# Two layer norms of a two-block transformer kernel rewoven: sums and centring from PSUM, a root by ScalarE, low parts by GpSimd alone, half-slab waits for TensorE

## What is computed

```python
x = _layer_norm(ALPHA * x + gate1 * y, ln1_g, ln1_b)        # y ends with "@ w_out"
h = x * (1.0 + scale2) + shift2
u = depthwise_conv3(h @ w_up) + conv_b                      # 5632 channels
gate, val = split(u, 2)
y = (silu(gate) * val) @ w_down
x = _layer_norm(ALPHA * x + gate2 * y, ln2_g, ln2_b)        # the output

def _layer_norm(x, g, b):
    mu = mean(x, -1); var = mean(square(x - mu), -1)
    return (x - mu) * rsqrt(var + 1e-5) * g + b
```

## Time and profile before

| | |
|---|---|
| median of 3 runs | 1785.66 us (1785.66 to 1786.78) |
| the profiled execution, its own time | 1783.52 us |
| its span, first to last instruction | 1781.4 us |
| mean granted PE clock | 0.997 |
| PE busy | 1748.0 us, 98% of the span |
| DVE, ACT, POOL busy | 972.4, 677.6, 825.1 us |
| DMA | 178.49 MB, 100 GB/s on average |

### The profile page before, as it was taken

How to read it: one execution, slowest core, us unless ns; L and a number is a source line. 1 busy time by engine, 2 the same in 40 slices (tenths; PEclk the granted TensorE clock), 3 DMA queues, 4 the chain that set the end, 5 groups by cost and what they waited for, 6 DMA issues and landing times. The chain is left out here.

```text
span 1781.4 us, 26139 instructions
## 1 busy us (share of the span) xinstructions
PE 1748.0 (98%) x8971; PEld 1485.4 (83%) x8971; DVE 972.4 (55%) x1592; ACT 677.6 (38%) x1399; POOL 825.1 (46%) x664
## 2 busy tenths in 40 slices
PE   8999999999999999999999999999999899999997
PEld 6888888888777888888888888999988878888886
DVE  4266535668975477252124359475577673551544
ACT  5322222243476433233233223665532552332333
POOL 4554454467971555544445555201034465444551
PEclk9999999999999999999999999999999999999999
DMA  7354452534312345433423333100022134323321
GB/s 230 108 180 138 142 154 83 179 96 116 89 34 60 117 142 184 145 95 95 124 78 100 107 95 99 44 1 25 1 59 83 48 101 136 101 88 107 94 83 48
DMA packets 279716, 178.49 MB, mean 100 GB/s; under 512 B 6280, under 2 KB 258372, under 8 KB 279492
## 3 DMA queue, kind: packets, MB, share of 16 engines
q1 hardware_dynamic: 265364, 149.35, 28.8%
q10 hardware_dynamic: 14256, 27.87, 4.5%
HBM read 175.11 MB, written 2.10 MB: 99 GB/s over the span
## 5 line engine op out<-in xcount | busy, mean ns | idle before, releaser
L655 POOL TENSOR_TENSOR wL<-raw,wH 128x512 fp32r<-128x512 f32 (+2 forms) x560 | 747.5, 1358 | 889.8 <-ACT wH L1443 798.9
L761 PE MATMUL ps<-actH,wH 128*128 128x512 f32 (+1 forms) x1312 | 511.0, 390 | 10.3 <-DVE actL L2417 3.8
L761 PE MATMUL ps<-actL,wH 128*128 128x512 f32 (+1 forms) x1312 | 504.5, 384 | 0.4 <-DVE actL L1872 0.4
L761 PE MATMUL ps<-actH,wL 128*128 128x512 f32 (+1 forms) x1312 | 504.1, 385 | 0.0
L1443 ACT ACTIVATE wH<-raw 128x512 fp32r<-128x512 f32 (+2 forms) x558 | 311.7, 609 | 335.8 <-PE ps L761 335.7
L761 PEld LDWEIGHTS ps<-actH,wH 128*128 128x128 f32 x1312 | 247.2, 188 | 62.4 <-issue 4.5
L761 PEld LDWEIGHTS ps<-actL,wH 128*128 128x128 f32 x1312 | 247.3, 188 | 49.5 <-DVE actL L1872 0.8
L761 PEld LDWEIGHTS ps<-actH,wL 128*128 128x128 f32 x1312 | 247.0, 188 | 49.1
L761 PE MATMUL ps<-hidH,wH 128*128 128x512 f32 (+1 forms) x720 | 267.7, 372 | 0.0
L761 PE MATMUL ps<-hidH,wL 128*128 128x512 f32 (+1 forms) x720 | 266.6, 370 | 0.0
L761 PE MATMUL ps<-hidL,wH 128*128 128x512 f32 (+1 forms) x720 | 266.5, 370 | 0.0
(11 more groups left out here) (341 smaller groups left out, 2075.9 us busy)
## 6 DMA issues: line engine op xcount, KB each, us to landing
mod_raw<-in_w_mod ACTq DMA_DIRECT2D x24, 1024.0 KB, 6.4
raw<-in_w_in SPq DMA_DIRECT2D x48, 512.0 KB, 3.7
raw<-in_ffn_w_up SPq DMA_DIRECT2D x44, 512.0 KB, 3.9
raw<-in_w_up SPq DMA_DIRECT2D x44, 512.0 KB, 3.8
raw<-in_ffn_w_gate SPq DMA_DIRECT2D x43, 512.0 KB, 3.9
raw<-in_ffn_w_down SPq DMA_DIRECT2D x32, 512.0 KB, 3.8
raw<-in_w_out SPq DMA_DIRECT2D x16, 512.0 KB, 3.6
raw<-in_w_down SPq DMA_DIRECT2D x16, 512.0 KB, 3.7
```

The lines of the kernel that those rows point to most:

```text
L655: nc.gpsimd.tensor_tensor(wL[:, b:b + w // 2], raw[:, b:b + w // 2], wH[:, b:b + w // 2].bitcast(F32), ALU.subtract).then_inc(lo_ready, 1)
L761: return nc.tensor.matmul(out, a, b, start=first, stop=last)
```

## The change

All of it is a new order and a new division of work; the products on PE are the same. In parts:

1. **Half-slab waits.** `feature_tiles` and `third_slabs` wait for the first half of a slab's low part before k = 0 and for the second half before the middle k.
2. **Table preloads.** Tiny activations (Silu, Sigmoid, Sqrt) are placed ahead of the stages that use these functions, among them Silu before the last eight `affine` and thus ahead of the `f3_up0` loop, and Sqrt before `merge` and before the end.
3. **The norm at the convolution.** `acc` starts as the sum of the four old tiles 4 to 7, so that `second_tile` adds each product straight from PSUM both to `x` and to `acc`; `add_half` goes. `centre` reads the provisional mean from PSUM (`PROVISIONAL = 4/3`), `rB` goes. The variance's root is `moment_root` on ACT plus four small DVE operations (`moment_scale`). `normal_two` weaves two tiles. All sixteen low parts are made by POOL, woven between its halves of the slabs 2 and 3. `moments(0)` moves from after (1, 0, k = 7) to after (1, 0, k = 4), `spread_moments(0)` from (1, 2, 7) to (1, 1, 5), `spread_moments(1)` one k earlier.
4. **The end.** The transposes of blocks 0 and 1 stand two k earlier; the first 256 columns of the second feature half of blocks 2 and 3 are summed and squared before the last transposes (`early_sums`, `squared_early`), only 256 columns after them; one `last_block` moves from behind the last transposes to before them; the ACT table for Sqrt is loaded ahead.

The core of the diff:

```diff
-    DVE_LOWS = 4
+    DVE_LOWS = 0
+    PROVISIONAL = 4.0 / 3.0
 ... POOL, f3_up0
-                    lows(st, 0)
-                    for n in range(DVE_LOWS, 2 * KT):
+                    lows(st, 0, slots=(0, 1))
+                    normal_low(0)
+                    lows(st, 0, slots=(2,), halves=(0,))
+                    normal_low(1)
+                    lows(st, 0, slots=(2,), halves=(1,))
+                    for n in (2, 3):
+                        normal_low(n)
+                    lows(st, 0, slots=(3,), halves=(0,))
+                    for n in range(4, KT):
+                        normal_low(n)
+                    lows(st, 0, slots=(3,), halves=(1,))
+                    for n in range(KT, 2 * KT):
                         normal_low(n)
 ... PE, feature_tiles
-                    pe.wait_ge(lo_ready, (i * 4 + (st["base"] + j + 1)) * 2)
                     pe.wait_ge(drained, i * 4 + (drain_base[name] + j - 3))
                     for k in range(K):
+                        if k in (0, K // 2):
+                            pe.wait_ge(lo_ready, i * 8 + ((st["base"] + j) * 2 + (1 if k == 0 else 2)))
 ... PE, last_down
-                if (half, j, k) == (1, 0, 3):
+                if (half, j, k) == (1, 0, 1):
 ... PE, third_slabs
-                        if (half, js, k) == (0, (3,), 1):
+                        if (half, js, k) == (0, (3,), 0):
                             spread_moments(1)
 ... PE, moments and the hooks of out2
-            pe.wait_ge(acc_done, ACC_TOTAL[2] + 4 * (half + 2))
+            pe.wait_ge(*((drained_v, drain_base["out2"] + KT) if half else (half_drained, 4)))
             pe.wait_ge(sq_added, 4 * (half + 2))
-                     lambda half, j, k: None if k < KT - 1 or half == 0 else
-                     moments(0) if j == 0 else spread_moments(0) if j == 2 else None)
+                     lambda half, j, k: moments(0) if (half, j, k) == (1, 0, 4) else
+                     spread_moments(0) if (half, j, k) == (1, 1, 5) else None)
 ... ACT, between out2 and f3
         split(third, 0, 0)
+        moment_root(0)
+        square(8)
         split(third, 0, 1)
-        square(8)
+        affine(0)
+        affine(1)
         square(9)
         split(third, 0, 2)
-        affine(0)
-        affine(1)
+        affine(2)
+        affine(3)
         square(10)
         split(third, 0, 3)
-        affine(2)
+        affine(4)
         square(11)
-        for n in range(3, 2 * KT):
+        for n in range(5, KT):
+            affine(n)
+        moment_root(1)
+        nc.scalar.activation(exp_of_zero[:], zero[:], ACT.Silu).then_inc(table_ready, 1)
+        for n in range(KT, 2 * KT):
             affine(n)
 ... DVE
-            V.tensor_tensor(part(dev, e), x[:, k * S + first:][:, 0:w], rB[:, first:first + w],
-                            ALU.subtract).then_inc(centred, 1)
+            V.scalar_tensor_tensor(part(dev, e), bank(4, w, first), PROVISIONAL, x[:, k * S + first:][:, 0:w],
+                                   ALU.mult, ALU.subtract).then_inc(centred, 1)
 ... second_tile
+            V.scalar_tensor_tensor(xh, src, modc[:, 16 + m:17 + m], xh, ALU.mult, ALU.add).then_inc(x_second, 1)
+            V.scalar_tensor_tensor(a, src, modc[:, 16 + m:17 + m], a, ALU.mult, ALU.add).then_inc(
+                drained_v if half else half_drained, 1)
 ... normal_two
+            for xh in xs:
+                V.tensor_tensor(xh, xh, bank(7, HS, half * HS), ALU.subtract).then_inc(less_mean, 1)
+            for m, xh in enumerate(xs):
+                dve.wait_ge(less_mean, n + m + 1)
+                V.tensor_tensor(xh, xh, bank(6, HS, half * HS), ALU.mult).then_inc(normed_x, 1)
 ... the end of the norm's order
         second_tile(1, 0)
+        moment_scale(0)
         centre(8)
+        dve.wait_ge(row_bcast, 4)
+        normal_two(0)
         second_tile(1, 1)
         centre(9)
 ... the end, DVE
+        last_block(1, 0)
+        half_tile("f3_down2", 1, 2, 40, 4)
+        early_sums()
+        last_block(1, 1)
         half_tile("f3_down2", 1, 3, 40, 4)
-        last_block(1, 0)
         dve.wait_ge(fin_T, 2 * ST)
-        turned_sum(3)
+        turned_sum(3, 256, rest, fin_copy)
         dve.wait_ge(fin_sq, ST + 3)
-        turned_sum(2)
+        turned_sum(2, 256, rest, fin_copy)
         dve.wait_ge(fin_copy, 2)
         final_mean(1)
+        gained_block(2, 0)
         final_var(1)
-        last_block(1, 1)
-        gained_block(2, 0)
+        gained_block(3, 0)
```

More of the change, by code:

```diff
@@ L343, in _build @@
     dev = at("dev", ("free", 10 * S), 2 * S)
+    early = at("early", ("free", 7 * S), S)
     ln2_gB = at("ln2_gB", ("kv", 0), D)
@@ L359, in _build @@
     late_gate = sem("late_gate")
+    table_ready = sem("table_ready")
     v_late = sem("v_late")
@@ L648, in _, with lows @@
             nc.gpsimd.memset(inv_w[:, g:g + 1], 1.0 / w).then_inc(cleared, 1)
-        def lows(st, i, then=None, slots=range(SLOTS)):
+        def lows(st, i, then=None, slots=range(SLOTS), halves=(0, 1)):
             for j in slots:
                 a, w = j * SLAB, st["width"]
-                for n, b in enumerate((a, a + w // 2)):
+                for n, b in [(n, a + n * (w // 2)) for n in halves]:
                     pool.wait_ge(hi_ready, i * 8 + ((st["base"] + j) * 2 + n + 1))
@@ L1718, in during2 @@
                 turned_high(TURN_AT[u])
+        nc.scalar.activation(exp_of_zero[:], zero[:], ACT.Sigmoid).then_inc(table_ready, 1)
         slabs("gates", 0, gate, last=last_gates)
@@ L1790, in copied, with squared, squared_early @@
                                  accum_out=ssq[:, (0, 20)[n // ST] + n % ST:][:, 0:1]).then_inc(fin_sum, 1)
-        def squared(n):
-            q = n % ST
-            if n >= 2:
-                act.wait_ge(fin_sq, n - 1)
-            nc.scalar.activation(tile(sq2, n % 2), bank(4 + q) if n >= ST else out_block(n), ACT.Square, scale=D ** -0.5,
+        SQUARES = (0, 1, ST, ST + 1, 2, 3, ST + 2, ST + 3)
+        def squared(n, first=0):
+            q, p = n % ST, SQUARES.index(n)
+            if p >= 2:
+                act.wait_ge(fin_sq, p - 1)
+            src = bank(4 + q, 512 - first, first) if n >= ST else out_block(n)
+            nc.scalar.activation(tile(sq2, p % 2)[:, first:], src, ACT.Square, scale=D ** -0.5,
                                  bias=ssq[:, 8 + q:9 + q], accum_out=ssq[:, 32 + n:33 + n]).then_inc(fin_sq, 1)
+        def squared_early(q):
+            nc.scalar.activation(early[:, q % 2 * 256:][:, 0:256], bank(4 + q, 256), ACT.Square, scale=D ** -0.5,
+                                 bias=ssq[:, 8 + q:9 + q], accum_out=ssq[:, 42 + q:43 + q]).then_inc(early_sq, 1)
         def deviation(pair):
@@ L1802, in deviation @@
                                  ACT.Sqrt).then_inc(fin_root, 1)
+        nc.scalar.activation(exp_of_zero[:], zero[:], ACT.Sqrt).then_inc(exp_begun, 1)
         for q in range(ST):
@@ L1806, in _ @@
         act.wait_ge(fin_mean, 1)
-        nc.scalar.activation(exp_of_zero[:], zero[:], ACT.Sqrt).then_inc(exp_begun, 1)
-        for n in range(ST):
-            squared(n)
-        for n in range(ST, ST + 2):
-            copied(n)
-        for n in range(ST, ST + 2):
-            squared(n)
-        deviation(0)
-        for n in range(ST + 2, 2 * ST):
-            act.wait_ge(fin_T, 2 * ST)
-            if n == 2 * ST - 1:
-                act.wait_ge(fin_copy, 1)
-            squared(n)
+        for q in range(2):
+            squared(q)
+        for q in range(2):
+            copied(ST + q)
+        for q in range(2):
+            squared(ST + q)
+        deviation(0)
+        for q in (2, 3):
+            squared(q)
+        act.wait_ge(fin_early, 2)
+        squared_early(2)
+        act.wait_ge(early_copy, 1)
+        squared_early(3)
+        act.wait_ge(fin_T, 2 * ST)
+        squared(ST + 2, 256)
+        act.wait_ge(fin_copy, 1)
+        squared(ST + 3, 256)
         deviation(1)
@@ L2413, in low @@
-        def low(n):
-            half, k = n // KT, n % KT
-            dve.wait_ge(shifted, n + 1)
-            dve.wait_ge(act_hi, 4 * KT + n + 1)
-            V.tensor_tensor(half_of(actL, k, half), aff[:, (n % 2) * HS:][:, 0:HS], half_of(actH, k, half).bitcast(F32),
-                            ALU.subtract).then_inc(act_ready, 1)
-        link(V.memset(acc[:], 0.0))
+            V.scalar_tensor_tensor(small[:, two], ps[:, 5, 4 + 2 * half:6 + 2 * half], LN_EPS, md[:, two],
+                                   ALU.add, ALU.subtract).then_inc(ln_var, 1)
@@ new lines, in moments, with moment_scale @@
+            dve.wait_ge(ln_var, half + 1)
+        def moment_scale(half):
+            two = slice(2 * half, 2 * half + 2)
+            y, v, a = bank(5, 2, 20), small[:, two], small[:, 64:66]
+            dve.wait_ge(ln_root, half + 1)
+            link(V.reciprocal(y, small[:, 16 + 2 * half:18 + 2 * half]))
+            link(V.tensor_tensor(a, v, y, ALU.mult))
+            link(V.scalar_tensor_tensor(a, a, -0.5, y, ALU.mult, ALU.mult))
```

(11 more changed lines are left out.)

115 lines of the change are left out of this document (56 added, 59 removed).

## The result

Over six runs of each, the median went from 1786.22 us (1784.84 to 1787.20) to 1776.22 us (1775.64 to 1776.56). The ratio is 0.9948, 95% interval 0.9938 to 0.9958, so 9.3 us gained with an interval of 7.5 to 11.1 (the two medians are 10.0 us apart). The forecast was a gain of 8.2 us and a median of 1777.5 us, range 1774.5 to 1782.0. The profiled execution of the changed kernel took 1776.10 us with a span of 1774.3.

A forecast was written before the change was run, and what follows sets the result against it. PE, busy 98% of the span, was taken to bound the kernel. Gains of 0.9 (half-slab waits), 4.0 (norm), 2.2 (second iteration) and 1.1 (end) sum to 8.2 us, median 1785.66 to 1777.5 us, range 1774.5 to 1782.0.

The forecast's parts named there:

- What bounds: Whole kernel: PE is busy 98% of the span, so other engines matter only where PE idles for them.
- Half-slab waits: Second iteration of the first up stage: PE's wait for `wL` goes, 0.92 us; the added mid-slab waits cost nothing.
- The norm: From half slab (1, 0) through the first f3_up0 iteration: 4.0 us gained, bounds 1.5 and 5.9.
- `moments(0)`: After k = 4 of half slab (1, 0): PE newly waits 0.7 us for the squares.
- first spread: After (1, 1, 5): PE waits 0.3 us for `rn`.
- low part 2: First f3_up0 iteration: POOL delivers at 1396.0, PE asks at 1395.1, wait 0.9 us.
- low part 4: First f3_up0 iteration: comes 2.9 us after part 2, PE asks after 2.16, wait 0.75 us.
- second half's start: Second token half of the first f3_up0 iteration: PE waits 0.9 us for its first low part.
- four times 0.4 us: Norm: POOL held by each of DVE's four `add_square`; gain 3.2 instead of 4.0 us at the least favourable meeting.
- the rest is the clock: First f3_up0 iteration: of PE's 7.8 us lost, 5.8 are gaps and 1.8 the clock granted at half.
- The second iteration's start: Start of the second f3_up0 iteration: PE's gap of 2.2 us goes; bound 1.3 us if the table load stays.
- The end: After PE's last transposes: shorter sums save 0.5 and one block fewer 0.66, 1.1 us; bounds 0.6 and 1.4.

The follow-up runs named there:

- experiment 6: Changed kernel with full-slab waits in feature_tiles, without the Silu preload ahead of the last eight affine passes, or with both undone: 1778.14, 1776.82 and 1780.69 us.
- experiment 7: Changed kernel with a wait ahead of each of the eight k per slab in feature_tiles instead of two: 1775.64 us.
- experiment 9: Changed kernel with moments(0) after k = 6: 1774.97 us; last kernel, that plus new POOL and ACT order, earlier root and moved spreads: 1773.42 us.
- Experiment 3: Kernel before with extra unused PE products ahead of the waits for low parts 0, 1 and 2 in the first up iteration: 1785.66 us, ratio 1.0000.
- experiment 1: Changed kernel again, unchanged, with a second profile: 1775.67 us, ratio to before 0.9945.
- experiments 2: Kernel before again, unchanged, with a second profile: 1784.63 us; its profiled execution took 1786.56 us.
- 4: Kernel before with 17 extra unused PE products filling the gap ahead of the second f3_up0 iteration: 1784.73 us, ratio 0.9994.
- 5: Kernel before with only the half-slab waits in feature_tiles and the Silu preload, old norm and end: 1781.52 us, ratio 0.9974.

## Why the forecast held, point by point

**What bounds.** Right. PE's busy time didn't move (1748.0 and 1747.5 us), and the gain that the trace shows lies in the four places.

**Half-slab waits**, 0.92 us forecast: right, and the row shows no wait at 37 us. The full waits of experiment 6 bring it back. The second wait in mid-slab costs nothing (experiment 7).

**The norm**, 4.0 us: 4.2 came. The stretch of the first up iteration was 7.8 us above its work and, by the rows, 1393.22 to 1420.66, 27.4 us less 24.8, is now 2.6 above it. Ahead of it, from the first matmul of (1, 0) to `out2`'s last one, PE takes 14.20 us instead of 13.16 (1378.54 to 1391.70): 1.0 us for the two waits there and the slower starts behind them. The waits one by one, from start to start less the pitch:

| place | forecast | measured |
|---|---|---|
| `moments(0)` | 0.7 | 0.66 |
| first spread | 0.3 | 0.18 |
| low part 2 | 0.9 | 0.64 |
| low part 4 | 0.75 | 0.84 |
| second half's start | 0.9 | 0.90 |

They sum to 3.2 against 3.6. The mis-sized term is POOL's time. The forecast took 1.43 us for half a slab and 0.74 for a low part; over the norm of the changed kernel they are 1.32 and 0.77:

```profile
L660 POOL TENSOR_TENSOR wL<-raw,wH 128x512 fp32r<-128x512 f32 x10 | 13.0, 1317 | 17.2 <-ACT wH L1462 17.2
L714 POOL TENSOR_TENSOR actL<-aff,actH 128x256 fp32r<-128x256 f32 x16 | 12.3, 769 | 7.9 <-ACT actH L1764 7.9
```

The shorter halves fit DVE reading more from PSUM, though no run here changes that alone. Collisions still occur, and all of them lie in POOL's chain ahead of low part 4. Here is that chain, and the four square additions of DVE, which have both inputs in SBUF:

```profile
1388.43 2.75 POOL L660 TENSOR_TENSOR wL<-raw,wH 128x512 fp32r<-128x512 f32 x2 [1.53 <-ACT wH L1462]
1391.14 0.74 POOL L714 TENSOR_TENSOR actL<-aff,actH 128x256 fp32r<-128x256 f32 x1
1391.84 1.30 POOL L660 TENSOR_TENSOR wL<-raw,wH 128x512 fp32r<-128x512 f32 x1
1393.09 0.92 POOL L714 TENSOR_TENSOR actL<-aff,actH 128x256 fp32r<-128x256 f32 x1
...
1395.23 1.62 POOL L714 TENSOR_TENSOR actL<-aff,actH 128x256 fp32r<-128x256 f32 x2
1396.81 1.30 POOL L660 TENSOR_TENSOR wL<-raw,wH 128x512 fp32r<-128x512 f32 x1
1398.07 0.90 POOL L714 TENSOR_TENSOR actL<-aff,actH 128x256 fp32r<-128x256 f32 x1
```
```profile
1389.39 0.63 DVE L2424 TENSOR_TENSOR sq<-sq,sq 128x256 f32<-128x256 f32 x1
...
1392.38 1.03 DVE L2424 TENSOR_TENSOR sq<-sq,sq 128x256 f32<-128x256 f32 x1
...
1395.78 0.47 DVE L2424 TENSOR_TENSOR sq<-sq,sq 128x256 f32<-128x256 f32 x1
...
1397.87 0.51 DVE L2424 TENSOR_TENSOR sq<-sq,sq 128x256 f32<-128x256 f32 x1 [0.30 <-ACT sq L1756]
```

Each addition took longer than the 0.42 us it takes alone. The one at 1392.38 ended behind POOL's half slab, and the POOL instruction that follows the one it met is longer each time: 1.49 instead of 1.30 us (the second of the pair at 1388.43), 0.92, 0.93 (the second of the pair at 1395.23) and 0.90 instead of 0.74. The rule of the Trainium skill, SBUF — State Buffer, section Who interferes with whom, that such a DVE instruction contends with a GpSimd one that reads SBUF, and that the lock is exclusive, agrees. Together POOL lost 0.7 us. That is about the size of the 0.8 that the forecast put beside its 4.0, although "four times 0.4 us" would be 1.6 and doesn't lead to that 0.8. It still didn't cost the gain, because the forecast's 1.43 us for each half was too long: up to low part 4, five halves took 6.7 us instead of 7.15 and five low parts 4.2 instead of 3.7. That two sizes wrong in opposite directions cancel there, and the wait for low part 4 comes out at 0.84 against 0.75, is luck; at low part 2, with fewer of the lengthened low parts ahead of it, the forecast is 0.26 too high.

That ACT's root buys little where it stood, behind a split that waits for PE, was right: `rn` was ready 6.79 us behind the first matmul of (1, 0) (1385.69), against 7.02 before (1385.56). The root ahead of that split is one part of the last kernel of experiment 9.

**The step that was wrong** is in the reading of the 7.8 us: "the rest is the clock ... cost 1.8 us". Experiment 3 keeps the clock up and gains nothing. The forecast survived because its gain came from following PE forward through the new order and not from adding what would go. Had I taken the waits and the clock as separate gains, one of the two would have been counted in vain.

**The second iteration's start**, 2.2 us: right for the gap, and its division between table load and half wait too (experiment 6). Not seen was what follows the gap in some executions: 3.4 us at half clock with operands ready, 1.6 us. The first profile of before, which the forecast rested on, had none. It also had an early start of the program, 1.1 us ahead of the changed kernel's profile and 1.3 ahead of the second one of before. Its time, 1783.52, was below all three runs shown. That difference of 2.1 us from the median was in the table ahead of the prediction, and the forecast carried it through as a constant. It wasn't one: the changed kernel's runs lie on its profile.

**The end**, 1.1 us: 1.0 by the runs, 1.15 by the trace. The two short sums start 0.60 us apart instead of the 0.49 worked out, since the second waits 0.17 us for ACT's square. The cover of 0.5 us ahead of the last gated half tile was there: DVE idled 0.64 us before it.

**The sum.** By the traces, place by place, 0.9 + 4.2 + 2.2 + 1.1 = 8.4 us against 8.2. The runs say 9.3 (7.5 to 11.1), and 9.8 in experiment 1. The 1 us between is of the sign and size of the second fall of the clock, by experiments 2, 4, 5 and 6 together. How often it comes in before isn't measured. A rival is the start of the program, which moves by over 2 us from one execution to another; but it favours neither kernel, since the matmul used as its mark above starts at 32.7 us on average in the five profiles of before and its variants and in the nine of the changed kernel and its variants. The interval of the ratio holds 8.4 as well, so this 1 us is argued and not shown.

**What wasn't separated.** The half waits, the preload and the end were each undone. The norm was not: its 4.2 us are what the traces show for part 3 as a whole, with each wait named. What the sums from PSUM, ACT's root, the woven pairs and the new places on PE give singly, no run tells.

## What to carry to other kernels

Follow the critical engine forward through the new order, wait by wait, and take the gain as the difference of two such timelines: subtracting a stall or a slow clock on its own counts time that the next wait takes back. When one profile stands well below the median of its kernel, look at a second one before trusting that it holds all that the change removes. A helper that feeds the critical engine should do its pieces in the order in which they are asked for: moving two 1.3 us pieces behind small ones that were due first gained, with the rest of that order, 2.3 us at no cost in work.

## What the runs showed of the hardware

In these runs a half clock cost time only where PE had work ready. In the norm of before, 3.4 us of it cost nothing (35.03 us with the clock up, 35.00 and 34.98 with it down, at two different places). Behind a gap of 2.2 us, with operands ready, the same 3.4 us cost 1.6 us (342.61 to 344.21 us for the same work). Of the four profiles with that gap unfilled three show the fall (the second one of before, the one with the norm's waits filled, the changed kernel with both parts undone) and one doesn't (the first of before).

DVE's addition of two tiles in SBUF and POOL's subtraction of two tiles in SBUF hold each other up. Four meetings in the norm lengthened the next POOL instruction by 0.16 to 0.19 us each (1.49 us instead of 1.30; 0.92, 0.93 and 0.90 instead of 0.74) and DVE's addition from 0.42 to between 0.47 and 1.03 us.

Satisfied waits on PE are free in this program: eight in each slab instead of two, and the time from one matmul's start to the next stayed at 0.227 us.
